# A two-block transformer kernel on one core: output tiles' blocks woven into the last inverse, a fourth tile beside the last states, weights split one unit further ahead

## The reference, cut to what matters

```python
# block 1: RWKV-7 time mixing + attention over a memory, output projection, FFN
h = rms_norm(x, norm_mix_g)
mix, q_mem = rwkv7_time_mix(h, ...)          # delta rule over 512 tokens, 12 heads of 64
mem_out = memory_cross_attention(q_mem, k_mem, v_mem, ...)
x = x + jnp.concatenate([mix, mem_out], -1) @ w_out        # 1024 x 1024
x = x + jnp.square(jax.nn.relu(rms_norm(x, norm_ffn_g) @ w_ff1)) @ w_ff2
# block 2: neighbourhood attention + sliding-window attention, gated, then a gated FFN
h = rms_norm_2(x, norm_mix_2)
...
x = x + y @ w_out_2
x = x + (silu(h @ w_gate) * (h @ w_up)) @ w_down
```

## Time and profile before

| | us |
|---|---|
| median of three runs | 1523.72 |
| lowest and highest | 1519.39, 1524.26 |
| the profiled execution | 1518.95 |
| its span | 1517.2 |
| TensorE busy | 1462.2 (96%) |
| VectorE, ScalarE, GpSimd busy | 800.4, 552.7, 239.4 |
| mean granted TensorE clock | 0.997 of full |

### The profile page before, as it was taken

The page is one execution under the profiler, slowest core; times in us unless marked ns, Lnnn a source line. Parts: engine busy times, 40 slices in busy tenths (PEclk is TensorE's granted clock), DMA queues, the critical chain, the costliest instruction groups (busy, mean ns, idle before and its releaser), DMA issues.

```text
span 1517.2 us, 26650 instructions
## 1 busy us (share of the span) xinstructions
PE 1462.2 (96%) x11374; PEld 1156.8 (76%) x11374; DVE 800.4 (53%) x1261; ACT 552.7 (36%) x942; POOL 239.4 (16%) x166
## 2 busy tenths in 40 slices
PE   7999999979999999999999999999999999999999
PEld 6867777756788888888788766767777888888887
DVE  5655566664564444535644358577554443443343
ACT  7444434363422221312442256545333221222221
POOL 0233333201200000000110012222322210220120
PEclk9999999999999999999999999999999999999999
DMA  8311011011223232333233133311222333323223
GB/s 323 112 30 44 30 30 44 23 52 58 70 87 108 84 108 87 98 97 97 84 97 96 58 107 96 94 56 53 83 92 89 97 97 98 97 85 109 84 88 107
DMA packets 39334, 130.89 MB, mean 86 GB/s; under 512 B 4272, under 2 KB 5296, under 8 KB 39216
## 3 DMA queue, kind: packets, MB, share of 16 engines
q1 hardware_dynamic: 39216, 129.18, 26.9%
HBM read 127.07 MB, written 2.10 MB: 85 GB/s over the span
## 4 chain that ended last, share of the span: by engine, by line
PE 82%; DVE 8%; ACT 4%; issue 3%; POOL 0%; POOLq 0%; ACTq 0%; DVEq 0%
PE bank L1047 79%; PE bank L1447 1%; DVE Wlo L1643 1%; ACT Whi L2090 1%; DVE qa L1754 1%; DVE z L1680 0%; DVE Xi L1886 0%; DVE qa L1752 0%; ACT Hhi L2171 0%; PE bank L1161 0%; DVE X L1725 0%; ACT kbr L2337 0%; ACT slab L2306 0%; PE bank L1237 0%; ACT tmpb L2205 0%
## 5 line engine op out<-in xcount | busy, mean ns | idle before, releaser
L1047 PE MATMUL bank<-Hhi,Whi 128*128 128x512 f32 x912 | 375.8, 412 | 11.6 <-DVE Wlo L1643 8.4
L1047 PE MATMUL bank<-Hhi,Wlo 128*128 128x512 f32 x912 | 360.9, 396 | 0.0
L1047 PE MATMUL bank<-Hlo,Whi 128*128 128x512 f32 x912 | 357.6, 392 | 0.0
L1047 PE MATMUL bank<-Uhi,Whi 128*128 128x512 f32 x736 | 290.9, 395 | 8.1 <-POOL Wlo L2418 3.1
L1047 PE MATMUL bank<-Uhi,Wlo 128*128 128x512 f32 x736 | 287.2, 390 | 0.0
L1047 PE MATMUL bank<-Ulo,Whi 128*128 128x512 f32 x736 | 287.0, 390 | 0.0
L2090 ACT CAST Whi<-Wraw 128x1024 fp32r<-128x1024 f32 (+1 forms) x216 | 222.9, 1036 | 164.2 <-PE bank L1047 148.2
L1643 DVE TENSOR_TENSOR Wlo<-Wraw,Whi 128x1024 fp32r<-128x1024 f32 (+1 forms) x175 | 224.2, 1282 | 98.9 <-ACT Whi L2090 98.8
L1047 PEld LDWEIGHTS bank<-Hhi,Whi 128*128 128x128 f32 x912 | 171.5, 188 | 66.0 <-issue 12.3
L1047 PEld LDWEIGHTS bank<-Hlo,Whi 128*128 128x128 f32 x912 | 171.9, 188 | 42.1
L1047 PEld LDWEIGHTS bank<-Hhi,Wlo 128*128 128x128 f32 x912 | 172.0, 189 | 34.0 <-issue 1.2
(11 more groups left out here) (292 smaller groups left out, 1571.8 us busy)
## 6 DMA issues: line engine op xcount, KB each, us to landing
Wraw<-in_wts SPq DMA_DIRECT2D x208, 512.0 KB, 3.5
bA<-in_biasA SPq DMA_DIRECT2D x12, 256.0 KB, 2.8
Wraw<-in_wts SPq DMA_DIRECT2D x8, 384.0 KB, 3.2
x<-in_xT SPq DMA_DIRECT2D x8, 256.0 KB, 4.4
x_rows<-in_xN SPq DMA_DIRECT2D x2, 1024.0 KB, 8.3
X<-in_xT SPq DMA_DIRECT2D x2, 1024.0 KB, 7.2
out<-X SPq DMA_DIRECT2D x8, 256.0 KB, 2.1
bB<-in_biasB SPq DMA_DIRECT2D x4, 384.0 KB, 3.1
```

The source lines that it names most:

```text
L1047: return e.matmul(o, lhsT, rhs, start=start, stop=stop, skip_group_check=True)
```

## The change

The filler beside `inverse(5)` gets a third generator, `early_blocks`: the first four blocks (slices 0 to 3) of the first and of the second output tile, in rotation with the states of p = 4 and with the memory's attention. `inverse(5)` is now blended by itself, with a factor of 1.2, and what is left of its filler is run before the load of X and before states(5). Beside states(5) and tail(5) then come the three other blocks of tiles 26 and 27 and seven blocks each of tiles 28 and 29, so that four tiles wait for slice 5. Tile 29 as well as 28 now holds one of the five small banks over that stretch. Behind it, `ahead` is 3 in place of 2 for all tiles to the end of the kernel.

```
-FILL_PAIR = (1.05, 1.35, 1.35, 1.35, 1.35)
+FILL_PAIR = (1.05, 1.35, 1.35, 1.35, 1.35, 1.2)
...
-    outs = [tile("res", ("gffn", i), ("wo", i), "mix", mix_order, js=mix_order, own=i == 2) for i in range(3)]
+    outs = [tile("res", ("gffn", i), ("wo", i), "mix", mix_order, js=mix_order, own=i >= 2) for i in range(4)]
+
+    def early_blocks():
+
+        for g in outs[:2]:
+            yield from spaced(itertools.islice(g, 4), 0.8)
+
+    filler = turns(itertools.chain(bonus(NP - 1), states(NP - 2), tail(NP - 2)), mem_att, early_blocks())
+    blend(inverse(NP - 1), filler, FILL_PAIR[-1])
+    run(filler)
+    step("Xload")
 
     def beside():
-        yield from turns(itertools.chain(bonus(NP - 1), states(NP - 2), tail(NP - 2)), mem_att)
-        step("Xload")
         for i, g in enumerate(outs):
 
-            state["ahead"] = (NW - 1, NW, NW - 1)[i]
-            yield from spaced(itertools.islice(g, 7), 0.8)
-        state["ahead"] = NW - 1
+            state["ahead"] = min(NW - 1, NW + 1 - i)
+            yield from spaced(itertools.islice(g, 3 if i < 2 else 7), 0.8)
+        state["ahead"] = NW
 
     filler = beside()
-    blend(itertools.chain(inverse(NP - 1), states(NP - 1, 0.6), spaced(tail(NP - 1), 1)), filler, FILL_LAST)
+    blend(itertools.chain(states(NP - 1, 0.6), spaced(tail(NP - 1), 1)), filler, FILL_LAST)
     run(filler)
     state["lo"] = "wlo"
 
     for i in range(8):
-        run(outs[i] if i < 3 else tile("res", ("gffn", i), ("wo", i), "mix", range(8), own=i == 3))
+        run(outs[i] if i < 4 else tile("res", ("gffn", i), ("wo", i), "mix", range(8)))
```

## The result

The changed kernel took 1524.8 us (median of 20 runs, 1524.15 to 1529.85), the kernel before 1522.3 us beside it (20 runs, 1518.93 to 1524.38). The ratio is 1.0024, with a 95% interval of 1.0016 to 1.0031: 3.7 us slower, within the 0.3% that count as no change. (The ratio compares all runs of both kernels; their medians alone lie 2.5 us apart.) The forecast was +5.0 us. The profiled execution took 1524.5 us, its span 1522.7 us. One execution of a later kernel, the profiled one of *three tiles*, took 5007 us; it is left out of that kernel's ratio, and has no stages in the table.

The account below looks back on a forecast made before the run. TensorE, busy 96% of the span, was taken to bound the kernel, so only its waits could yield time. Terms: 3.5 - 1.2 + 1.3 + 2.1 + 1.5 - 2.2 = +5.0 us on 1523.72, giving 1528.7 us, range 1519 to 1535.

Parts of the forecast that it names:

- C: Stage from pd(5) to the first block for slice 5, 21.4 us: two blocks more, +1.3 us (+1.1 to +1.8).
- D: Stage from slice 5's first block to tile 30's first matmul, 9.8 us: split behind one more eviction, +2.1 us.
- A: Stage from inverse(5)'s first scores to xu(5, 4), 47.8 us: eight blocks added, about half hidden, +3.5 us (0 to +7.1).
- B: Stage from xu(5, 4) to pd(5), 10.2 us: three blocks fewer against new waits, -1.2 us (-2.7 to +1.5).
- root's wait of 1.2 us: In B, TensorE's wait at root t(4): claimed to go, 1.2 us saved.
- The clock behind tile 30: After D's idle time, some 3 us of matmuls at half clock take twice as long: +1.5 us (0 to +3).
- The later stages: Tile 30 to the end, `ahead` at 3: some waits for `Wlo` go, -2.2 us (0 to -9).
- the bound that the prediction had set as a sign of being wrong: Prediction counts as wrong if the stretch behind tile 30 shrinks by more than 4 us.
- Order: The moved blocks without the lookahead, around the last inverse up to behind tile 30: forecast +7.2 us.
- blocks in A not hidden: Rival, chance 0.17: the eight blocks in A cost 7.1 us in place of 3.5, total 1532.3 us.
- all hidden and the clock stays up: Rival, chance 0.18: A's idle 10.5 us take all eight blocks, tile 30 runs at full clock; 1523.7 us, no change.
- the lookahead pays: Rival, chance 0.15: waits for `Wlo` among `both` tiles and attention really go, 9.2 us won; 1521.7 us.

Follow-up runs that it names:

- three tiles: Changed kernel with three output tiles ahead of slice 5 instead of four, tile 29 whole behind them, early blocks and lookahead kept: 1522.5 us, ratio 1.0010 to before.
- order-alone: Changed kernel with `ahead` left at 2, so only the moved blocks remain of the change: 1529.3 us, ratio 1.0048 to before.
- early split: Changed kernel with the split of unit 30 put behind tile 26's eviction instead of tile 29's: 1521.6 us, ratio 0.9999 to before.
- no early blocks: Changed kernel without the eight blocks beside the inverse; seven blocks of each of the four tiles stand beside the states: 1537.0 us, ratio 1.0103 to before.
- rate 1.0: Changed kernel with the filler factor beside the last inverse at 1.0 instead of 1.2: 1528.5 us, ratio 1.0043 to before.
- The experiment that removed this drop: Changed kernel with 30 unused matmuls of 512 columns right ahead of tile 30 to keep TensorE at work: 1526.5 us, ratio 1.0029 to before.
- the lookahead alone: Kernel before with `ahead` at 3 instead of 2 behind the output projection, old order kept: 1518.3 us, ratio 0.9982 to before.

## Why the prediction was right

**C and D** came as forecast: C +1.16 us (+1.3), D +2.03 (+2.1), with one idle time of 8.88 us (9.1), put down to VectorE's `Wlo`. That it is the place of the split in the list is shown: moved forward, it leaves 5.1 or 4.0 us of D, and 2.2 or 1.1 us of the wait. (The 1.6 us for two blocks in C is neither 2 x 0.89 nor 2 x 0.69; the term came out all the same.)

**A and B** were forecast at +2.3 together and measured at +3.3. In the profile after, the clock fell at 357 to 360 us within B. The order-alone kernel and the one with the early split have the same list there and no such drop: 59.7 us in both. Seven profiles have the new order in A and B: five with the drop in B (61.0 to 61.9 us) and two without it, 60.80 us in the mean. Three have the old order (57.94, 58.96 and 58.45), 58.45 in the mean. So the term is +2.35 in the mean, as forecast, and between +0.7 and +4.0, by where the clock falls. The drop has moved: all three with the old order have one in A, none of the seven has, and in the five it comes at the two waits of 1.2 and 1.3 us for z. The forecast took 0 for the first, and did not see the second. The split into A +3.5 and B -1.2 can't be checked, as the change moves root and tn over the bound. One piece of B was wrong: root's wait of 1.2 us did not go. Before, it stood at 349.67 us, ahead of B's start, so it was no part of B to be saved; after, it is in the list above as it was, and in B. The 0.5 us forecast ahead of uw did not come. The rest of the mechanism (blocks partly hidden, waits of other kinds in B) shows in the list of waits. What I did not see is that the blocks were no addition that one could as well leave out. Without them A and B grow by 2.7 us where the expectation of that run took off 3.5; the sum was right for the whole change, but not each of its parts taken alone.

**The clock behind tile 30** was forecast at +1.5 with 0 to +3, and cost 2.65 us. The mechanism was right, and the size was near the upper bound: the clock was down for 5.6 us of matmuls, not 3. Three more profiles have the same wait of 8.9 us, and there the clock behind it cost 1.9 (order alone), 1.8 (no early blocks) and 2.2 us (rate 1.0). The rule of the Trainium skill that was named there ("TensorE: Matmul & The Clock Gate", "Why this matters for your kernels") had the direction right; it speaks of longer pauses than most of those at which the clock fell here. The experiment that removed this drop won its 2.65 us in the trace, but not in the median; so the term is shown in profiled executions only.

**The later stages** were forecast at -2.2 with 0 to -9. Measured: -4.0 in the profile (9.58 to 5.55 us behind), -2.7 (1.2 to 4.3) by the lookahead alone. The 4.0 lies at the bound that the prediction had set as a sign of being wrong (more than 4 us). Among the `both` tiles nothing stayed of the waits for GpSimd, as argued from the earlier trace rows; at the first attention items the 1.6 us won were lost again at the next step, which now waits 2.2 us for VectorE. The gain is in many small pieces that I had put at "a few tenths": 1.6 us between 740 and 780 us, over five starts of tiles of 0.2 to 0.5 us each, 0.9 between 1144 and 1192, 0.9 in the last stretch.

**Sum.** Order +7.2 forecast, +7.3 measured; lookahead -2.2 forecast, -2.7 measured. That the total came out at +3.7 and not +5.0 lies within the intervals of the parts. Between the two profiles it is +5.55: 0.5 ahead of A, 3.3 + 1.2 + 2.0 + 2.65, less 4.0. The misses of single terms (+1.0 in A and B, +1.15 for the clock, -1.8 later) nearly cancel, which is luck. Two things of the forecast did not come true. It held slower (0.49) likelier than the same (0.39), and the same came. And the time it gave, 1528.7 us, is 3.9 us above the 1524.8 measured, which lies just under its own 1525 to 1532, though within the whole range of 1519 to 1535. Of the 3.9 us, 1.4 are the base (the median of three runs, 1523.72, against 1522.3 of twenty), the rest the change. Of the rivals, "blocks in A not hidden" would have made A and B 5.9 us longer, more than any of the seven profiles shows, "all hidden and the clock stays up" fell with the 8.88 us wait and the half clock behind it, and "the lookahead pays" with the waits of the `both` tiles.

## What to carry to other kernels

Blocks that run while a set of results is evicted are cover, and worth more there than in an idle stretch elsewhere: before moving them away, look for what stands behind the evictions in the other engines' lists, here one split, and move that first. That move and the lookahead, in the old order, made the kernel 0.5% faster, where the reordering made it 0.5% slower. A wait taken away from an engine that is ahead of its consumer comes back at the next step. And where buffers are handed out in rotation, any reordering changes who gets whose: follow the rotation to the long-lived holders before costing an order.

## What the runs showed of the hardware

The clock falls at short waits too, and not each time: behind 2.18 us of idle in the early-split kernel, behind the same 2.23 us at 907 us in one execution and not in another, and not behind the 1.83 us of the earlier trace rows. In the thirteen profiles that can be compared, the wait of 2.2 us that all have between 1016 and 1037 us comes with a drop in nine. The eleven with the lookahead wait 2.2 us between 898 and 917 us, and 1.8 us between 1105 and 1127 us; each of these waits comes with a drop in five of them. Such a drop lasted some 3 us and cost 1.5 us at the two places where it was compared (908 and 1116 us); the one of the 8.9 us wait lasted from 394.4 to 404.7 us.

The scatter between executions goes with this. The kernel before took 1519.2 us in its 8 executions at a mean granted clock of 0.997, and 1522.6 in 15 at 0.994 (medians of the third session); the changed one 1524.5 us in 11 at 0.993, and 1529.8 in 3 at 0.989. A single profile can therefore be 3 to 5 us off its kernel's median (the profile before is 3.4 us under it, and the slowest run of the changed kernel 5.0 above), and of a change of 0.2% the parts must be read from stretches in which both clocks are the same.
